# A decoder layer step on one core: the sample's cross-attention front moved into the mixer's last turns, and the last tile's token table ahead of its gates

## The reference

```
h = rmsnorm(x); q, k, v, ua, ub = split(h @ w_in)
x = x + concat(window_attention(q, k, v), swish(layernorm(causal_conv31(ua * sigmoid(ub))))) @ w_out
q = rmsnorm(rmsnorm(x) @ w_mq) per head            # 4 heads of 256
x = x + softmax(q @ mem_k.T / 16) @ mem_v @ w_mo   # 256 memory positions
h = rmsnorm(x); top-1 of 4 groups, top-2 of its 8 experts
x = x + sum over the two experts of gate * (silu(h @ w_gate) * (h @ w_up)) @ w_down
```

## Time and profile before

| | |
|---|---|
| device time, median of 3 runs | 1385.19 us (1384.43 to 1388.69) |
| the profiled execution | 1390.01 us, of which the span is 1387.8 |
| TensorE busy | 1231.1 us, 89% of the span |
| VectorE / ScalarE / GpSimd busy | 715.1 / 311.8 / 156.8 us |
| HBM read and written | 187.17 MB and 46.56 MB |

### The profile page before, as it was taken

One profiled execution on the slowest core, in us unless ns is written; L12 is line 12 of the kernel. 1 busy time (PEld: TensorE's weight loads), 2 busy tenths in 40 slices (PEclk: granted clock), 3 DMA queues, 4 the chain that ended last, 5 costly groups with the idle time before them and its releaser, 6 DMA issues. The chain is left out here.

```text
span 1387.8 us, 17739 instructions
## 1 busy us (share of the span) xinstructions
PE 1231.1 (89%) x6455; PEld 632.0 (46%) x6455; DVE 715.1 (52%) x2214; ACT 311.8 (22%) x891; POOL 156.8 (11%) x173
## 2 busy tenths in 40 slices
PE   7978979999999938687999999998759999999992
PEld 3444554555555423453555666655423433333330
DVE  2118799999999984331345554455434422222210
ACT  1134334534535341120111111111001111101100
POOL 0000000000000000100000000000012333333322
PEclk9988899999999968897999999999869999999996
DMA  8860000300000040373114200003368999999952
GB/s 319 289 211 20 0 24 0 153 31 1 31 31 16 1 149 31 140 276 122 31 46 187 86 16 31 31 31 121 144 258 328 383 360 391 376 375 378 367 155 37
DMA packets 52367, 207.35 MB, mean 149 GB/s; under 512 B 14160, under 2 KB 17142, under 8 KB 38435
## 3 DMA queue, kind: packets, MB, share of 16 engines
q1 hardware_dynamic: 39611, 186.27, 34.9%
q0 software_dynamic: 12096, 17.88, 5.5%
q10 hardware_dynamic: 576, 2.10, 0.4%
HBM read 187.17 MB, written 46.56 MB: 168 GB/s over the span
## 5 line engine op out<-in xcount | busy, mean ns | idle before, releaser
L806 PE MATMUL bank<-W,G 128*128 128x512 f32 (+1 forms) x768 | 314.0, 564 | 3.7 <-DVE G L1656 2.9
L1712 DVE SCALAR_TENSOR_TENSOR W<-W,dwT 128x128 f32<-128x128 f32 (+1 forms) x1080 | 280.0, 335 | 0.0
L806 PEld LDWEIGHTS bank<-W,G 128*128 128x128 f32 x768 | 145.2, 192 | 150.5 <-issue 147.1
L1256 PE MATMUL bank<-W 128*32 128x512 f32 x1264 | 199.8, 600 | 4.1 <-issue 2.4
L1030 PE MATMUL bank<-W 128*128 128x512 f32 x256 | 116.5, 614 | 10.6 <-ACT W L1502 6.7
L2134 DVE TENSOR_TENSOR W<-bank,cvec 128x512 f32<-128x512 f32 x56 | 36.2, 686 | 164.0 <-PE bank L1243 163.9
L682 POOL TENSOR_SCALAR st<-st 128x1 f32<-128x1 f32 (+3 forms) x41 | 8.0, 196 | 935.9 <-DVE st L1795 470.1
L1205 PE MATMUL bank<-W 128*128 128x512 f32 x256 | 113.3, 595 | 0.2 <-DVE W L2021 0.2
L1256 PEld LDWEIGHTS bank<-W 128*32 128x32 f32 x1264 | 59.4, 115 | 104.1 <-issue 101.7
L1263 PE MATMUL bank<-W 128*32 128x512 f32 x632 | 101.6, 595 | 0.5 <-ACT W L1604 0.5
L1030 PEld LDWEIGHTS bank<-W 128*128 128x128 f32 x256 | 49.7, 197 | 72.1 <-issue 71.8
(11 more groups left out here) (297 smaller groups left out, 1549.1 us busy)
## 6 DMA issues: line engine op xcount, KB each, us to landing
W<-in_w_exp_gate SPq DMA_DIRECT2D x29, 1024.0 KB
W<-in_w_exp_up SPq DMA_DIRECT2D x29, 1024.0 KB
W<-in_w_exp_down SPq DMA_DIRECT2D x29, 1024.0 KB
W<-in_cache_mem_k SPq DMA_DIRECT2D x8, 1024.0 KB, 5.7
W<-in_cache_mem_v SPq DMA_DIRECT2D x8, 1024.0 KB, 7.2
W<-in_w_in SPq DMA_DIRECT2D x4, 1792.0 KB, 25.4
G<-in_w_exp_gate SPq DMA_DIRECT2D x7, 1024.0 KB
G<-in_w_exp_up SPq DMA_DIRECT2D x7, 1024.0 KB
```

The lines of the kernel that those rows point to most:

```text
L806: mm = pe.matmul(bank[0:rows, at:at + hi - lo], HT[:, c, 0:rows], w[:, c, lo:hi], start=(c == 0), stop=(c == DC - 1))
L1256: mm = pe.matmul(B[2 + par][lo:hi, :], HG[par][:, c, lo:hi], WGU[u][:, :, c, :], start=(c == 0), stop=(c == DC - 1), skip_group_check=True)
L1712: dve.scalar_tensor_tensor(y, src, w, y, ALU.mult, ALU.add).then_inc(M["conv_tap"], 1)
```

## The change

1. The sample's tile 0 gets its second norm, its product with `w_mq`, the norm of its queries, their turning and their spread into `QP2` in the mixer's turns 8 (norm), 9 (product) and 10 (turning). The cross-attention's loops begin at turn 1.
2. A new `turn_early(b)` turns the keys of sequences 0 and 1 in the mixer's turn 10, around tile 8's variance. ACT copies all eight banks. The loop over b then turns only sequences 2 to 7; sequence 0 is scored before anything is turned.
3. For that the names of the token buffers are turned by one in the cross-attention (`XB(s)` is `XR[(s + 3) % 4]`), and the loads of x1 from DRAM stand in other turns. In turn 9 one transposed half of the probabilities goes to bank 2 in place of 4.
4. `route_rows` puts the token numbers and the one-hot rows in front of the gates. For the last tile PE adds only the token table before the indices are placed; `last_gates` adds the gates behind.
5. SP loads slot 5 only when the first two gathers have landed.

The diff, cut to its core:

```diff
+        def XB(s):
+            return XR[(s + 3) % 4]
...
+        QN2_S = view(G, 8192, MH, MHD)
+        QT2_S = HT[:, :, 0:NS]
...
-                if s3 == 6 or s3 == 7:
-
-                    s = s3 - 6
-                    sp.wait_ge(x1_out[s], 32)
-                    sp.dma_start(XR[s][0:rows_of(s), :], tok_rows(x1_d, s)).then_inc(x1_in[s], 16)
+                if 5 <= s3 <= 7:
+
+                    s = s3 - 5
+                    sp.wait_ge(x1_out[(s + 3) % 4], 32)
+                    sp.dma_start(XB(s)[0:rows_of(s), :], tok_rows(x1_d, s)).then_inc(x1_in[s], 16)
 
             sp.wait_ge(M["wo_done"], 2 * NT)
-            sp.wait_ge(M["x_sq"], NT + 3)
+            sp.wait_ge(M["x_sq"], NT + 4)
...
-                if 2 <= it + 2 < NT:
-                    k = (it + 2) % 4
+                if 3 <= it + 2 < NT:
                     if it + 2 == 3:
-                        sp.wait_ge(x1_out[3], 32)
-                    sp.dma_start(XR[k], tok_rows(x1_d, it + 2)).then_inc(x1_in[k], 16)
+                        sp.wait_ge(x1_out[2], 48)
+                    sp.dma_start(XB(it + 2), tok_rows(x1_d, it + 2)).then_inc(x1_in[(it + 2) % 4], 16)
...
                     for k in range(4):
                         sp.wait_ge(x2_out[k], 16 * len(range(k, NT, 4)))
+                    sp.wait_ge(zg_in[0], 16)
+                    sp.wait_ge(zg_in[1], 16)
...
+                if it == NT:
+                    pool.wait_ge(M["q2_ssq"], AFTER["q2_ssq"] + 1)
+                    rsqrt(st[0:NS, 32:36], st[0:NS, 36:40], "q2_rs", 1.0 / MHD)
+                    pool.memset(QP2, 0.0).then_inc(M["qp2_zero"], 1)
+            norm_x(NT + 3, rows_of(1))
...
+            def turn_early(b):
+
+                pe.wait_ge(mk_in[b], 16)
+                for mt in range(2):
+                    if mt == 0 and b:
+                        pe.wait_ge(M["mk0_ready"], 2)
+                    if mt == 1:
+                        pe.wait_ge(M["mk0_ready"], 4) if b else pe.wait_ge(M["q2T_ready"], AFTER["q2T_ready"] + 2)
+                    for half, done in enumerate(("mkb_tA", "mkb_tD")):
+                        for c in range(4):
+                            k = 4 * half + c
+                            mm = pe.transpose(B[(2 if mt else 4) + half][:, c * 128:(c + 1) * 128], MKB[b][:, mt, k * 128:(k + 1) * 128], ident)
+                        mm.then_inc(M[done], 1)
...
+                if s1 == NT:
+                    pe.wait_ge(M["ptA_ready"], copies_before(s1 - 1))
+                    pe.wait_ge(M["ptD_ready"], s1 - 1)
+                    pe.wait_ge(M["u_ready"], s1)
+                    turn_z(NT + 2, NS, (5, 4))
...
-                elif s3 >= 0:
+                elif s1 == NT:
+                    pe.wait_ge(M["wmq_in"], 64)
+                    pe.wait_ge(M["s_ready"], 8 * NT)
+                    for mm in sample_pair((B[4], 0, 512, w_mq), (B[5], 512, 1024, w_mq)):
+                        mm.then_inc(M["mq_done"], 1)
                     ln_variance(s3)
+                    ln_spread(s3)
+                else:
+                    pe.wait_ge(M["q2n_ready"], AFTER["q2n_ready"] + 2)
+                    pe.wait_ge(M["ptA_ready"], copies_before(NT))
+                    for half in range(2):
+                        for c in range(4):
+                            k = 4 * half + c
+                            mm = pe.transpose(B[2 + half][:, c * 128:c * 128 + NS], QN2_S[0:NS, k // 2, (k % 2) * 128:(k % 2) * 128 + 128], ident[0:NS, 0:NS])
+                        mm.then_inc(M["q2T_done"], 1)
+                    turn_early(0)
+                    ln_variance(s3)
+                    turn_early(1)
                     ln_spread(s3)
...
-                        if b:
-                            pe.wait_ge(M[got], AFTER[got] + 2 * b + mt - 1)
+                        if b > 2:
+                            pe.wait_ge(M[got], AFTER[got] + 2 * (b - 2) + mt - 1)
+                        elif mt == 0:
+                            pe.wait_ge(M["mk0_ready"], 8)
...
+                if s4 < NT - 1:
+                    pe.wait_ge(M["r_gates"], s4 + 1)
+                cols = 2 if s4 < NT - 1 else 1
                 for k in range(2):
-                    mm = pe.matmul(B[3][:, 64:64 + 2 * NE], RR[0:n4, k, :], RQ[0:n4, k, :, :], start=(k == 0), stop=(k == 1))
+                    mm = pe.matmul(B[3][:, 64:64 + cols * NE], RR[0:n4, k, :], RQ[0:n4, k, 0:cols, :], start=(k == 0), stop=(k == 1))
                 mm.then_inc(M["r_table"], 1)
 
+            def last_gates():
+
+                pe.wait_ge(M["r_gates"], NT)
+                for k in range(2):
+                    mm = pe.matmul(B[6][:, 0:NE], RR[:, k, :], RQ[:, k, 1, :], start=(k == 0), stop=(k == 1))
+                mm.then_inc(M["r_gtable"], 1)
...
-                        pe.wait_ge(M["q2T_ready"], AFTER["q2T_ready"] + 2)
                         pe.wait_ge(M["qp2_ready"], DEC_B)
-                        pe.wait_ge(M["ht_ready"], 2 * (s1 + NT + 3))
-                        turn_memory(0)
+                        pe.wait_ge(M["mk0_ready"], 8)
                         for b in range(DEC_B):
-                            if b + 1 < DEC_B:
+                            if b == 1:
+                                pe.wait_ge(M["ht_ready"], 2 * (s1 + NT + 3))
+                            if 1 <= b and b + 1 < DEC_B:
                                 turn_memory(b + 1)
-                            pe.wait_ge(M["mkbA_ready"], AFTER["mkbA_ready"] + 2 * b + 2)
-                            pe.wait_ge(M["mkbD_ready"], AFTER["mkbD_ready"] + 2 * b + 2)
+                            if b >= 2:
+                                pe.wait_ge(M["mkbA_ready"], AFTER["mkbA_ready"] + 2 * b - 2)
+                                pe.wait_ge(M["mkbD_ready"], AFTER["mkbD_ready"] + 2 * b - 2)
...
+                if s2 == NT:
+                    for b in range(2):
+                        for mt in range(2):
+                            for half, done in enumerate(("mkb_tA", "mkb_tD")):
+                                act.wait_ge(M[done], AFTER[done] + 2 * b + mt + 1)
+                                act.activation(MKTB[b][:, 4 * half:4 * half + 4, mt * 128:(mt + 1) * 128],
+                                               B[(2 if mt else 4) + half][:, :].rearrange("p (c t) -> p c t", c=4), ACT.Copy).then_inc(M["mk0_ready"], 1)
...
+                if s1 == NT:
+                    act.wait_ge(M["zt_done"], 2 * (NT + 3))
+                    for half in range(2):
+                        act.wait_ge(M["mq_done"], AFTER["mq_done"] + half + 1)
+                        act.activation(Z[0:NS, 512 * half:512 * half + 512], B[4 + half][held(0, half), :], ACT.Square).then_inc(M["q2_sq"], 1)
...
+                    if nxt == NT:
+                        act.wait_ge(x1_in[0], 16)
+                        sum_sq(NT + 2, NS, XB(0))
+                        root_x(NT + 2, NS)
...
+                if s1 == NT:
+                    dve.wait_ge(M["pua_done"], AFTER["pua_done"] + NT)
+                    take_hT(NT + 2, NS, V_XA, (5, 4))
...
+                if s2 == NT:
+                    for half in range(2):
+                        dve.wait_ge(M["q2T_done"], AFTER["q2T_done"] + half + 1)
+                        for r in range(2):
+                            c = 4 * half + 2 * r
+                            a = dve.tensor_tensor(QT2_S[:, c:c + 2, :], B[2 + half][:, 256 * r:256 * r + 256].rearrange("p (c t) -> p c t", c=2)[:, :, 0:NS],
+                                                  gain(V_MQ, 2, NS), ALU.mult)
+                        a.then_inc(M["q2T_ready"], 1)
+                    dve.wait_ge(M["qp2_zero"], 1)
+                    dve.wait_ge(M["q2T_ready"], AFTER["q2T_ready"] + 2)
+                    for b in range(DEC_B):
+                        dve.tensor_copy(QP2[:, b, :, DEC_T * (b % 4):DEC_T * (b % 4) + DEC_T], QT2_S[:, :, b * DEC_T:(b + 1) * DEC_T]).then_inc(M["qp2_ready"], 1)
...
+                    if s1 + 1 == NT:
+                        norm_z(NT + 2, NS, XB(0))
...
+                if s1 == NT:
+                    dve.wait_ge(M["q2_sq"], AFTER["q2_sq"] + 2)
+                    dve.tensor_reduce(st[0:NS, 32:36], Z[0:NS, :].rearrange("p (h d) -> p h d", h=MH), X, ALU.add).then_inc(M["q2_ssq"], 1)
+                    conv_taps(s2, CUTS[3], CUTS[4])
+                    dve.wait_ge(M["q2_ssq"], AFTER["q2_ssq"] + 1)
+                    dve.wait_ge(M["q2_rs"], AFTER["q2_rs"] + 1)
+                    for half in range(2):
+                        dve.tensor_tensor(QN2_S[0:NS, 2 * half:2 * half + 2, :], B[4 + half][held(0, half), :].rearrange("p (h d) -> p h d", h=2),
+                                          bc(st[0:NS, 36 + 2 * half:38 + 2 * half], MHD, 2), ALU.mult).then_inc(M["q2n_ready"], 1)
...
-                dve.wait_ge(M["r_exp"], AFTER["r_exp"] + s4 + 1)
-                link(dve.tensor_scalar(part[:, 2:3], part[:, 1:2], 1.0, part[:, 0:1], ALU.add, ALU.mult))
```

(19 more changed lines are left out.)

85 lines of the change are left out of this document (35 added, 50 removed).

## The result

| | before | after |
|---|---|---|
| median (range), six runs each | 1383.35 us (1380.79 to 1388.69) | 1374.24 us (1372.73 to 1376.71) |
| ratio after/before, 95% interval | | 0.9928 (0.9911 to 0.9945) |
| profiled execution: time, span | 1390.01, 1387.8 us | 1376.71, 1374.7 us |

The change made the kernel faster by 0.7%: 9.1 us between the medians, 13.3 us between the two profiled executions. The forecast was 10.4 us of saving and a median of 1374.8. The page of the changed kernel has TensorE busy for the same time: no work went away, only holes.

What follows compares the result with a forecast made beforehand. TensorE's program plus its holes bounds the kernel. W +4.7, the loop -11.2, routing -0.3 and the gather -3.6 sum to -10.4 us: from the median 1385.19 to 1374.8 us, range 1369 to 1381.5.

Steps and rivals of the forecast that it cites:

- the loop behind W: Sample's cross-attention loop after tile 8's output product: ends at W + 43.1 instead of W + 54.3, 11.2 us saved.
- W: End of tile 8's output product in the mixer, at 562.71 before; forecast to move 4.7 us later.
- Rival (e): Sample's loop: third keys still wait for their buffer, so W + 50 and no net change; chance 0.09.
- Turn 9: Mixer turn with tile 8's scores: query product hidden in an 8.54 us hole, next LayerNorm product 1.8 us late.
- The scaling: VectorE's 64-row scaling in turn 9, put at 1.76 us, the longer of two values shown.
- Turn 10: Mixer's LayerNorm chain before tile 8's output product: query and key transposes and copies cost 2.9 us, bounds 0 and 8.
- (a): Mixer's last two turns lose more, W moves 8 to 10 us, net about -6, 1379 us; chance 0.14.
- (d): Sample's front not hidden in turn 10, 20 us go into W, net +5, 1390 us; chance 0.06.
- The output product: Tile 8's, 16.12 us long: busier links could give back up to 2.1 us; none was counted.
- rival (c): Keys land early or clock stays up: 14 and 2 us saved, not 11 and 0; net -15, 1370; chance 0.13.
- Gather: Expert stage's first gather: rows 3.6 us earlier with three fewer weight loads ahead, bounds 1.5 and 4.5.
- rival (b): The gather is late by its own queue and gains nothing: net -7, 1378 us; chance 0.08.

Runs made afterwards that it cites:

- the doubled product: Changed kernel with the sample's query product done twice in turn 9: 1379.80 us, ratio 0.9944 to the kernel before.
- the move alone: Changed kernel with the old routing order and without the sixth slot's wait for the first two gathers: 1377.74 us, ratio 0.9937 to the kernel before.
- The square: Changed kernel with two sequences' keys turned in the loop or in turn 10; ratios to before: weights first 0.9933, 0.9928; keys first 0.9882, 0.9816.
- the version above: Changed kernel with the six later sequences' key loads asked for ahead of the output weights: 1360.13 us, ratio 0.9816 to the kernel before.

## Why the prediction was right

The step that carries it, the loop behind W, holds. Its sum was W + 43.1, with the third keys at W + 17.8 and 25.3 us from there on; measured were W + 41.3, W + 17.6 and 23.7. That the new stall is a queue of bytes, not of buffers or of turning, was argued from one window and is shown by the wait that stayed at W + 17.8 when other keys stood there, and by its fall to W + 4.6 with the order reversed. Rival (e), that the keys' buffer isn't free before W, is out by the same runs.

Point by point:

- **Turn 9.** Predicted 1.8 us, measured 1.10. The query product is hidden, as said, and the doubled product prices the cover. Two terms were off, in opposite directions. The scaling: I took the longer of its two values, 1.76 us. It took 0.74 (it had no zeroing beside it), the wait before the scores shrank from 2.52 to nothing, and VectorE took tile 8's scores up at 489.01 in both kernels, not 1.5 us late. With that shift gone, the sum would have given about 0.3. But the taps ended 4.86 us later (537.82 for 532.96) and not 4.0, for VectorE also waited 0.98 us for GpSimd's power in front of the normalisations, which the sum left out:

```profile
525.91 1.41 DVE L1939 TENSOR_TENSOR G<-bank,st 64x512 f32<-64x512 f32 x2 [0.98 <-POOL st L691]
```

- **Turn 10.** Predicted 2.9 us, measured 1.90 in the changed kernel's profile: 1.1 from the query work, 0.8 from the keys' transposes and copies. In four of the other five profiles with the same turn it was 3.4 to 3.6, so the forecast lies between what this turn costs at either clock. Rivals (a) and (d), that the front isn't hidden there, didn't occur. ScalarE's eight copies ended at 546.27 and its next step began at 546.46, when VectorE released it: the cover was used up to 0.2 us.
- **The output product.** I took nothing for its length; it gave back 0.45 us. That is this execution's value: with the same turn 10 it ran from 15.45 to 17.04 us, before 16.12. So W's 2.55 us is the smallest of six: with turn 9's 1.10, the others come to between 3.4 and 5.6, and the 4.7 of the forecast lies between them.
- **The loop.** 1.9 us more was saved than forecast, and only 0.2 of it by an earlier landing. The rest is the way from the third keys to the end, 23.7 us for 25.3: I had kept the old pace, with its wait of 2.60 us, and that wait did not come back. The hole itself was 11.52 us and not some 14, since TensorE was done with tile 1's turning and the first scores at W + 6.1, not W + 4; as the landing ends it, that cost nothing. Of rival (c), 14 saved in the loop, 13.1 came.
- **Behind the loop.** Not in the sum: the clock rose earlier in the sample's output product, which ran 8.05 us for 9.61, and 1.2 us of that reached the routing.
- **Routing.** Predicted 0.3, measured 0.39.
- **Gather.** Predicted 3.6, measured 3.27, and 2.5 to 4.3 over all profiles; rival (b) didn't occur. By turns between the rows of the queues (the Trainium skill, DMA: Bandwidth & Descriptors, Queues, rings and completion order) 2.3 had been worked out; that lies just outside the range. In all four profiles with the slot's loads ahead, the gathers' queue moved nothing for four us behind the issue, and then moved its first packets beside the last of the weights for one to two us. That is later than turns from the start would have it, and the measurement decides. The view sums the 16 engines, so whether each of them let all its weights pass first stays open.
- **The expert stage.** I said that what is saved reaches the end. Of 15.4 us at the gather's rows 2.3 were lost by the end: the first gate-and-up product took 10.03 us where it had 9.15, and the block behind the late wait 8.77 where it had 7.07, both with the granted clock at its lower level for part of the time. The late wait itself was 2.1 us (before 2.37). TensorE's row of that block in the changed kernel, and two windows there (columns as in the earlier trace rows):

```profile
1308.01 8.77 PE L1307 MATMUL bank<-W 128*32 128x512 f32 x64 [2.08 <-issue]
```

```profile
1306.00:1308.00 2.00, 0.00 (x0) 0.02 (x1) 1.26 (x2) 0.00 (x0) 1.70 (x2) 1.00 1.08 229
...
1310.00:1312.00 2.00, 2.00 (x16) 0.66 (x12) 0.00 (x0) 0.00 (x0) 0.00 (x0) 0.50 1.03 350
```

  The slot's postponed load is not the cause: the block took 8.7 us also with the move alone, which has no such wait. What decides between 7.07 and 8.7 stays open; the length of the wait does not (7.07 behind 2.58 us without early keys, 8.74 behind 2.14 with the move alone). It took 8.7 in four of the eleven profiles that have this wait, so the runs don't show that these 1.7 us are a price of the change.

So +1.1 +1.9 -0.45 for W, -13.06 for the loop, -1.2 behind it, -0.4, -3.3 and +2.3 make -13.1, against -10.4 predicted. That is the difference of two profiled executions, of which before's lies 6.7 us over its median and after's 2.5; the medians differ by 9.1, and 4 us between the two measures are scatter that no row explains. That the forecast median of 1374.8 came within 0.6 us of the measured 1374.24 is in part luck: it was counted from 1385.19, which three more runs moved to 1383.35, and the terms of the sum erred both ways.

What the prediction didn't see is how little of the move did the work. It put 11.2 us on taking work out from behind W. The square shows that turning two sequences' keys in the mixer gave 0.3 of it, and cost at least 0.8 in turn 10; the rest is the query work alone. The prediction had named the queue as what is late next, and stopped there: some 15 us more lay in the order of the key loads and the output weights.

## What to carry to other kernels

When work is moved out from in front of a chain of loads, look at what the queue holds at the new moment: the loads that used to be asked for late now meet a bulk load that was harmless before, and the order of the two becomes the price of the stage. A part of a change whose removal changes nothing may be worth much once the next bound is gone, so test parts in pairs, as a square, and not one by one. And where a trace shows two durations for one form, ask what ran beside the longer before choosing one.

## What the runs showed of the hardware

**VectorE beside GpSimd.** The scaling of 1024 columns from the on-chip buffer takes 0.74 to 0.75 us, but 1.76 or 1.77 wherever the zeroing of 1.80 us runs beside it, for 64 partitions as for 128. In the version above the zeroing ends at 565.15 and the scaling at 565.70, so it ends 0.55 us after, as if it had stood behind it; the zeroing loses nothing. The evacuations from the accumulation banks beside the other zeroing kept their length (two 64x512 in 1.41 us at 525.91 of the changed kernel, with the zeroing at 525.75; 1.40 before). The Trainium skill (SBUF — State Buffer, SBUF: two separate sides) says that the two engines share a pair of ports as an exclusive lock, which whichever starts first holds for its whole instruction; on VectorE's side this holds for instructions in a 2-port perf mode, or with two inputs from the on-chip buffer beside a GpSimd instruction that reads it. The trace agrees, with the 1.77 against 0.74 us; that the scaling runs in such a mode no row shows.

**The clock in a hole.** Windows of the changed kernel and of the version with all keys first; us, busy times, granted clock, DMA share, GB/s:

```profile
575.00:580.00 5.00, 0.00 (x0) 0.00 (x0) 0.00 (x0) 0.00 (x0) 0.00 (x0) 0.50 1.02 414
```

```profile
575.00:580.00 5.00, 4.92 (x52) 4.00 (x56) 2.09 (x4) 2.25 (x4) 0.00 (x0) 1.00 0.77 282
```

In the hole, which began at 571.35, the granted clock was at 1.00 from 572 to 574 and fell to 0.50 (1.2 GHz of 2.4) by 576; it had been there once before, from 568 to 571, after the wait of 2.52 us. The first 16 transposes behind the hole took 3.65 us instead of 1.97. Where the loop kept running, so did the clock, and no group was slow.
